# Fox attention of a one-core Trainium2 kernel: new step lists for the last two pairs of heads, and the first output unit closed behind three shares of the second

## What is computed

```
q = q * HEAD_DIM ** -0.5                        # 16 heads of 64
c = cumsum(log_sigmoid(f_logit))                # forget gate, per head
s = q @ k.T + c[query] - c[key], causal         # 512 x 512 scores
o = softmax(s) @ v
m = o @ w_out                                   # w_attn_out, 1024 x 1024
x = x + rmsnorm(m); then the first MLP of the layer
```

## Time and profile before

| what | value |
|---|---|
| time of three runs | 1836.65, 1836.42, 1834.61 us; median 1836.42 |
| the profiled execution's own time | 1832.28 us |
| its span | 1830.5 us |
| PE busy | 1757.6 us, 96% of the span |
| DVE, ACT, POOL busy | 1068.9, 740.6, 180.0 us |
| pair 6, pair 7 on PE | from 682.59 to 705.03 us, from 705.03 to 729.25 us |
| output product on PE after the lists | units a and b to 745.6 us, unit 2 from 748.61 us |

### The profile page before, as it was taken

One profiled execution on the slowest core, in us unless ns is written; L12 is line 12 of the kernel. 1 busy time (PEld: TensorE's weight loads), 2 busy tenths in 40 slices (PEclk: granted clock), 3 DMA queues, 4 the chain that ended last, 5 costly groups with the idle time before them and its releaser, 6 DMA issues.

```text
span 1830.5 us, 21934 instructions
## 1 busy us (share of the span) xinstructions
PE 1757.6 (96%) x8332; PEld 1448.3 (79%) x8332; DVE 1068.9 (58%) x1397; ACT 740.6 (40%) x1076; POOL 180.0 (10%) x144
## 2 busy tenths in 40 slices
PE   8999999999899998999999999979998999999987
PEld 6978877888688887768888887768886888888866
DVE  6367777676556776484435353776556635444475
ACT  4256764665425666351212123642124312222245
POOL 2000110000300000130000001430004000000041
PEclk9999999999999999999999999989999999999999
DMA  7222123214223221222332222322321333222221
GB/s 238 92 69 69 37 69 95 63 54 138 70 81 93 69 70 42 81 92 94 99 106 92 92 92 81 104 69 92 102 79 64 119 103 99 92 92 94 96 65 57
DMA packets 164702, 160.26 MB, mean 88 GB/s; under 512 B 13873, under 2 KB 157518, under 8 KB 164366
## 3 DMA queue, kind: packets, MB, share of 16 engines
q1 hardware_dynamic: 164622, 159.16, 27.8%
HBM read 150.36 MB, written 4.19 MB: 84 GB/s over the span
## 4 chain that ended last, share of the span: by engine, by line
PE 69%; issue 13%; DVE 7%; POOL 5%; ACT 4%; DMA 2%; SPq 0%; POOLq 0%; DVEq 0%; ACTq 0%
PE bank L749 21%; PE bank L751 21%; PE bank L750 21%; POOL ssum L2404 3%; PE bank L1009 2%; PE bank L1021 1%; DVE split_weights L1737 1%; DVE work L1796 1%; POOL tmp L2437 1%; DVE act_a L1783 1%; ACT split_weights L1248 1%; DMA raw_weights<-in_w_mlp_up 1%; DMA raw_weights<-in_w_ple_gate 1%; ACT sq L1278 1%; POOL ssum L2408 0%
## 5 line engine op out<-in xcount | busy, mean ns | idle before, releaser
L749 PE MATMUL bank<-act_a,split_weights 128*128 128x512 f32 x1392 | 558.0, 401 | 32.6 <-DVE act_a L1783 24.1
L751 PE MATMUL bank<-act_a,split_weights 128*128 128x512 f32 x1392 | 547.9, 394 | 0.0
L750 PE MATMUL bank<-act_a,split_weights 128*128 128x512 f32 x1392 | 547.8, 394 | 0.0
L1248 ACT ACTIVATE split_weights<-raw_weights 128x2048 fp32r<-128x2048 f32 (+1 forms) x118 | 221.8, 1880 | 335.8 <-PE bank L751 335.7
L1737 DVE TENSOR_TENSOR split_weights<-raw_weights,split_weights 128x2048 fp32r<-128x2048 f32 (+1 forms) x118 | 273.2, 2316 | 123.1 <-ACT split_weights L1248 119.7
L749 PEld LDWEIGHTS bank<-act_a,split_weights 128*128 128x128 f32 x1392 | 264.0, 190 | 96.5 <-issue 23.1
L751 PEld LDWEIGHTS bank<-act_a,split_weights 128*128 128x128 f32 x1392 | 263.8, 190 | 57.7
L750 PEld LDWEIGHTS bank<-act_a,split_weights 128*128 128x128 f32 x1392 | 264.4, 190 | 53.6 <-issue 2.2
L749 PE MATMUL bank<-act_b,split_weights 128*128 128x512 f32 x664 | 260.4, 392 | 0.0
L750 PE MATMUL bank<-act_b,split_weights 128*128 128x512 f32 x664 | 258.4, 389 | 0.0
L751 PE MATMUL bank<-act_b,split_weights 128*128 128x512 f32 x664 | 258.4, 389 | 0.0
(11 more groups left out here) (191 smaller groups left out, 2073.8 us busy)
## 6 DMA issues: line engine op xcount, KB each, us to landing
raw_weights<-in_w_mlp_up SPq DMA_DIRECT2D x32, 1024.0 KB, 5.4
raw_weights<-in_w_mlp_down SPq DMA_DIRECT2D x32, 1024.0 KB, 5.1
raw_weights<-in_w_in SPq DMA_DIRECT2D x20, 1024.0 KB, 5.3
raw_weights<-in_w_conv_in SPq DMA_DIRECT2D x12, 1024.0 KB, 5.1
raw_weights<-in_w_attn_in SPq DMA_DIRECT2D x16, 512.0 KB, 4.7
raw_weights<-in_w_ple_gate SPq DMA_DIRECT2D x8, 1024.0 KB, 5.1
raw_weights<-in_w_out SPq DMA_DIRECT2D x4, 1024.0 KB, 5.1
raw_weights<-in_w_attn_in SPq DMA_DIRECT2D x4, 1024.0 KB, 5.5
```

The costliest lines, as they stand in the source:

```text
L749: nc.tensor.matmul(dst, w[0], a[0], start=first, stop=False)
L750: nc.tensor.matmul(dst, w[0], a[1], start=False, stop=False)
L751: mm = nc.tensor.matmul(dst, w[1], a[0], start=False, stop=last)
L1248: nc.scalar.activation(wsp[:, pl.slot, 0, pl.split_cols], raw[:, pl.slot, pl.raw_cols], ACT.Copy)\
```

## The change

The four NEAR and LAST lists of PE, ACT and DVE (six lists in all) are written anew, with the same steps in another order; `w` and `c` stand earlier in them. `mixer_out` takes two shares of unit b, `turn_p`, a third share of b, share 7 of a, and then shares 3 to 7 of b. And `split_share` counts up a new semaphore `w_begun` with ACT's first half, so that DVE's `c0` and `c1` wait for the first half alone and `c2` for the second; this holds for all pairs of Fox and MLA.

```diff
--- before.py
+++ after.py
@@ -333,7 +333,7 @@
             ATT[kind] = {n: sem(f"{kind}_{n}") for n in (
                 "stage_hi", "staged", "scores", "turned", "clipped", "softplus", "masked", "part_hi",
                 "part_ready", "summed", "w_exp", "negmax", "exp", "normed", "pt_hi", "pt_ready",
-                "v_hi", "v_staged", "out", "sum_log", "sum_inverse", "gathered", "gated", "o_hi", "o_ready")}
+                "w_begun", "v_hi", "v_staged", "out", "sum_log", "sum_inverse", "gathered", "gated", "o_hi", "o_ready")}
         halves_copied = [sem("halves_copied0"), sem("halves_copied1")]
 
         block = ctx.enter_context(nc.Block())
@@ -384,14 +384,14 @@
         DVE_FOX = "m0 m1 c0 c1 m2 y0 p0 m3 m4 p1 c2 s2 c3 p2 p3 m5 m6 m7 y1 p4 p5 g0 p6 p7 x0 x1 s3 g1"
 
 
-        PE_NEAR = "z0 g0 z1 z2 g1 t0 g2 t1 t2 z3 z4 z5 g3 t3 z6 g4 v0 t4 g5 t5 g6 z7 g7 t6 t7 v1"
-        ACT_NEAR = "y0 e0 y1 e1 e2 p0 p1 e3 p2 p3 w0 e4 e5 r0 p4 w1 p5 e6 e7 p6 p7 s2 r1"
-        DVE_NEAR = "m0 m1 m2 y0 p0 m3 p1 p2 p3 m4 m5 y1 g0 c0 m6 p4 m7 p5 x0 x1 p6 p7 c1 s2 c2 g1 c3"
-
-
-        PE_LAST = "z0 z1 z2 g0 t0 z3 t1 g1 z4 t2 z5 g2 t3 z6 g3 t4 z7 v0 t5 g4 t6 t7 g5 g6 v1"
-        ACT_LAST = "o0 s1 o1 e0 w0 e1 p0 y0 o2 e2 p1 o3 e3 o4 p2 e4 p3 w1 o5 e5 o6 y1 e6 p4 p5 e7 r0 p6 p7 r1"
-        DVE_LAST = "o0 m0 m1 o1 s1 m2 p0 o2 m3 p1 m4 m5 y0 o3 o4 p2 p3 m6 c0 m7 c1 o5 p4 p5 c2 y1 o6 g0 p6 p7 g1 c3"
+        PE_NEAR = "z0 z1 z2 g0 g1 t0 t1 z3 g2 z4 t2 z5 g3 t3 z6 g4 t4 t5 v0 g5 z7 g6 g7 t6 t7 v1"
+        ACT_NEAR = "y0 e0 e1 p0 p1 e2 w0 w1 e3 p2 p3 e4 e5 e6 p4 p5 y1 r0 e7 p6 p7 s2 r1"
+        DVE_NEAR = "m0 m1 m2 m3 p0 y0 c0 c1 p1 p2 m4 m5 p3 m6 c2 p4 y1 m7 p5 g0 x0 x1 p6 p7 c3 s2 g1"
+
+
+        PE_LAST = "z0 z1 z2 t0 z3 g0 t1 g1 t2 g2 t3 z4 z5 z6 g3 t4 z7 g4 v0 t5 g5 t6 t7 g6 v1"
+        ACT_LAST = "o0 o1 e0 s1 p0 e1 y0 e2 o2 e3 p1 o3 w0 p2 y1 o4 p3 e4 o5 w1 e5 o6 e6 e7 p4 p5 r0 p6 p7 r1"
+        DVE_LAST = "m0 o0 m1 m2 o1 p0 m3 s1 o2 y0 p1 o3 c0 p2 m4 o4 y1 p3 o5 m5 c1 m6 m7 c2 c3 p4 p5 o6 g0 p6 p7 g1"
 
         ACT_MLA_LAST = "e0 e1 y1 p0 e2 p1 w0 e3 p2 p3 w1 e4 e5 p4 o0 e6 p5 o1 e7 p6 r0 p7 o2 r1"
         DVE_MLA_LAST = "m0 m1 m2 m3 p0 p1 p2 m4 p3 m5 c0 c1 c2 y1 m6 p4 c3 m7 p5 o0 p6 g0 o1 p7 x0 x1 o2 g1"
@@ -1106,12 +1106,13 @@
                     begun = sum(w == "g" for w, _ in steps(PE_LAST))
                     a, b = (Place(tab, name, j) for j in range(2))
                     b_banks = [bank(b, m) for m in range(2)]
-                    for share in range(begun):
+                    for share in range(2):
                         beside(b, share, tab.extra[name], ready[0], b_banks)
                     turn_p()
+                    beside(b, 2, ready=ready[0], dst=b_banks)
                     for share in range(begun, KT):
                         beside(a, share, ready=ready[0])
-                    for share in range(begun, KT):
+                    for share in range(3, KT):
                         beside(b, share, ready=ready[0], dst=b_banks)
                     project_normed(name, x, first=2)
                 else:
@@ -1248,15 +1249,14 @@
                 nc.scalar.activation(wsp[:, pl.slot, 0, pl.split_cols], raw[:, pl.slot, pl.raw_cols], ACT.Copy)\
                     .then_inc(w_hi, 1)
 
-            def split_share(pl, share):
+            def split_share(pl, share, begun):
 
                 if share == 0:
                     act.wait_ge(raw_landed[pl.slot], pl.landed)
                     act.wait_ge(tile_done, pl.freed)
                 cols = slice(share * UNIT // 2, (share + 1) * UNIT // 2)
-                hi = nc.scalar.activation(wsp[:, pl.slot, 0, cols], raw[:, pl.slot, cols], ACT.Copy)
-                if share:
-                    hi.then_inc(w_hi, 1)
+                nc.scalar.activation(wsp[:, pl.slot, 0, cols], raw[:, pl.slot, cols], ACT.Copy)\
+                    .then_inc(w_hi if share else begun, 1)
 
             def split_half(name, j, half):
 
@@ -1509,7 +1509,7 @@
                                 act.wait_ge(tile_read, here.tile)
                             stage_values(kind, pair + s // 2, s % 2, A["v_hi"])
                         elif what == "w":
-                            split_share(ahead, s)
+                            split_share(ahead, s, A["w_begun"])
                         elif what == "o":
                             output_hi(kind, s)
                         elif what == "r":
@@ -1737,9 +1737,11 @@
                 V.tensor_tensor(wsp[:, pl.slot, 1, cols], raw[:, pl.slot, pl.raw_cols], wsp[:, pl.slot, 0, cols].bitcast(F32),
                                 ALU.subtract).then_inc(w_split, 1)
 
-            def split_share(pl, share):
+            def split_share(pl, share, begun):
 
                 if share == 0:
+                    dve.wait_ge(*begun)
+                elif share == 2:
                     dve.wait_ge(w_hi, pl.u + 1)
                 cols = slice(share * UNIT // 4, (share + 1) * UNIT // 4)
                 lo = V.tensor_tensor(wsp[:, pl.slot, 1, cols], raw[:, pl.slot, cols], wsp[:, pl.slot, 0, cols].bitcast(F32),
@@ -2122,7 +2124,7 @@
                         elif what == "m":
                             maxima(pair, s)
                         elif what == "c":
-                            split_share(ahead, s)
+                            split_share(ahead, s, (A["w_begun"], pair + 1))
                         else:
                             turned_lo(pair, s)
 
```

## The result

The changed kernel takes 1820.95 us (median of 6 runs, 1819.67 to 1821.85) beside 1836.14 us of the kernel before (6 runs, 1834.61 to 1836.65). The ratio is 0.9919, with a 95% interval of 0.9906 to 0.9932: 14.9 us less, 12.5 to 17.3.

The account below looks back on a forecast made before the run. The prediction took PE as the bound, with gain only where it waits or its clock falls. Terms of 3.0, 3.2, 0.5 and 0 summed to 6.7 us, from the median 1836.42 to 1829.7 us; range 1825.8 to 1833.0.

Parts of the forecast that it names:

- Term A: Behind pair 7's last v1: c3 placed ahead of p4 lets unit b start at once; 3.0 us gained.
- Term B: In mixer_out: unit a closed early, five shares of b cover the wait ahead of unit 2; 3.2 us gained.
- Term C: Seam of pairs 6 and 7: shorter waits less new small ones; 0.5 us gained in sum.
- the walk: Step-by-step timing of the new lists of pairs 6 and 7; found new waits of some 0.3 and 0.5 us.
- Term D: Clock fall in pair 7: between 0 and 1.7 us to gain; 0 taken.
- rival 1: The clock does not fall in pair 7: gain 8.4 us, 1828.0 us; chance 0.30.
- The added waits: One more DVE wait per pair, for w_begun, over twelve pairs: 0.8 us at most, 0 taken.
- Rival 2: Share 7 of a comes before tile 7 is ready, holding b's shares 3 to 7: 1832.7 us; chance 0.10.
- Rival 3: Gain taken back at the first MLP's loads, or hidden by scatter: no change, 1836.4 us; chance 0.08.
- Rival 4: Earlier splits in pairs 6 and 7 hold ACT's and DVE's chain: 3.1 us slower, 1839.5 us; chance 0.05.

Follow-up runs that it names:

- e7: The changed kernel with DVE's c3 of the last pair put back at the end of its list; 1824.61 us, ratio to before 0.9945.
- e3: The kernel before with the new order of shares in mixer_out alone; 1829.94 us, ratio to before 0.9973.
- e4: The changed kernel with the old order of mixer_out; 1825.39 us, ratio to before 0.9946.
- e6: The changed kernel with w_begun waited for in pairs 6 and 7 only, elsewhere c0 waits for both halves; 1823.21 us, ratio to before 0.9935.
- e8: The changed kernel, unedited, measured again as a reference; 1821.24 us, ratio to before 0.9922.
- e9: The changed kernel with share g7 of pair 6 laid between t7 and v1; 1820.29 us, ratio to before 0.9924.
- e11: The changed kernel with g7 of pair 6 behind t7, o0 split in pair 6 and g0 ahead of t0 in pair 7; 1820.0 us, ratio 0.9919.
- e12: The changed kernel with share 0 of unit a in pair 6 between t7 and v1, pair 7 beginning with share 1; 1821.64 us, ratio 0.9921.
- e13: The kernel before with 45 useless matmuls laid into three PE stalls, ahead of pair 7's first share, unit b and unit 2; 1833.0 us, ratio 0.9987.
- e2: The kernel before with the semaphore w_begun alone, old lists and old mixer_out; 1832.9 us, ratio to before 0.9987.
- the control: An unchanged copy of the kernel before, measured beside it; 1835.34 us, ratio 0.9997.
- e5: The kernel before with m2 moved ahead of c0 and c1 in DVE_FOX, no new semaphore; 1834.4 us, ratio 0.9993.

## Why the prediction was right or wrong

**Term A (3.0 us): right.** The distance from the last `v1` matmul to unit b went from 3.13 to 0.12 us. e7 gives the wait back by moving `c3` alone.

**Term B (3.2 us): right.** Unit 2 starts 3.2 us sooner behind b's last matmul, and tile 7 is ready in time: no wait on it between b's shares. e3 takes only this edit and loses the wait, e4 gives it back (3.1 us).

**Term C (0.5 us): right in size.** The seam stall is 1.72 us (forecast 1.7), the copy's wait is gone, `g2` waits 0.3 us as the walk found. Two small items came out otherwise. The wait of `v1` in pair 6 stays whole (forecast 0.2 less), and the pair is 0.1 us shorter elsewhere. `v1` of pair 7 lost 0.24 us (forecast 0.5): it starts 0.47 us behind its forerunner instead of 0.23, of which 0.07 us show as idle. The load of unit 2 went 8.5 us sooner by the clock of the span, of which some 4 us are the shorter stretches ahead of it.

**Term D (0 taken, 1.7 us kept for the range): wrong, rival 1 was the case.** A stall of 1.72 us in the same place left the clock up, here and in e4, e6, e7, e8 and e9; the falls of e11 (700.5 us) and e12 (709.4 us) came behind other stalls, of 1.84 and 2.16 us. But the reason why 1.7 us could be won is not the prediction's. It counted 0.07 x 24.2 us as lost to the fall; by e13 the old order lost nothing by it, because the copy of head 15 held PE just as long. The 1.7 us became free only because the change also moved that copy out of the way.

**The added waits (0 taken): right.** With twelve waits more the MLA pairs take 21.95 us as before, and no Fox pair is longer by more than 0.02 us.

**The step that failed is in the paragraph on the added wait: "the earlier quarters in the MLA pairs and Fox pairs 0 to 5 can give back little, because PE waits there for 0.2 us and 0.4 us. I take 0 for this too".** For the MLA pairs it held (21.95 us a pair in both). For Fox pairs 0 to 5 it cost 3.0 us: e2 gains them with the semaphore alone, e6 loses them without it there. The waits of PE are not a bound on what it loses, since a matmul is drawn 0.39 us long at a distance of 0.23. The number to read was the length of a pair: in the trace of before the distance from pair 0 to pair 1 is 20.60 us and each later one 21.2 to 21.4, with the same lists. The 12.3 us of DVE's idle in the earlier trace rows pointed at the place, but not at the price: six of the ten cases are Fox pairs with 1.49 us each, of which pair 0 loses nothing, three are MLA pairs with 0.96 us each, which lose nothing, and the last is 0.5 us in pair 6.

**The second step is the base: "That execution was 4.1 us faster than the median of the runs, and I put the change against the median".** The prediction took the gain to be the same against both. It was not. The profiled execution had one of the three falls that the control shows, and neither profile of the changed kernel has any there. The two that the trace of before did not show are 3.4 us. Neither step alone takes the time out of the range: 6.7 + 3.0 us gives 1826.7 us. With rival 1 as well it is 1825.0 us, and with the two falls 1821.6 us, beside 1820.95 measured.

**The sum.** A 3.0, B 3.2, C 0.5, the early pairs 3.0, three falls about 5.1: 14.8 us, against 14.9 measured (12.5 to 17.3). From the profiles the same: pair 7 to the 3850th matmul 60.5 - 48.7 = 11.7 us (from the unrounded values) against the control, of which A, B, C's 0.3 in pair 7 and the falls are 11.6. The sum needs three falls in the median execution of before; with the one of the profiled execution it is 11.4 us, and the two profiles, of before and of after, are 11.6 us apart. So the number of falls is the least certain term. e13 seems to speak against counting the first fall, since it was swallowed by the copy there; in the changed kernel that wait is gone, and the gain of its removal is the same 1.7 us under another name.

**The rivals.** Rival 2: tile 7 was in time. Rival 3: the stretch behind unit 2 took back 0.7 us, not the gain, and even those can't be told from scatter: in the profiles of e1 to e12 that stretch takes 1067.9 to 1069.5 us, with the old lists and the new. Rival 4: PE's shares covered the earlier splits; in pair 7's window ACT was busy 18.60 us of 25 and DVE 17.54, and the only new waits of PE are the small ones named under term C.

**What stays open.** Why the same stall brings a fall in one execution and not in another: before and its copy have the same three waits, and one and three falls. How often which number comes was not counted, since only profiled executions show it; so the clock's part of the gain rests on one execution each of the control, e13 and the edits, and on two of the changed kernel. The lists of pairs 6 and 7 without the semaphore were not tried: with the old wait `c0` at its new place would need ACT's second half, which stands behind steps that wait for it.

## What to carry to other kernels

Where matmuls are pipelined, read what PE loses from the distances of starts, and compare stretches that have the same list: a pair that takes 21.3 us where its neighbour takes 20.6 has 0.7 us to give, whatever the waits say. When an engine stands idle at a wait and the next steps of the critical engine come from behind that wait in its queue, look at a finer semaphore too: here it gave 3.0 us in the trace, where moving one step past the wait gave 0.5 us, because the work behind the wait then came late for the next step. And before a profiled execution is used as the base of a sum, look at what it did differently from the median: each of the two long stalls was here worth 3 us of waiting and up to 1.7 us of clock, and the profile showed a fall at one stall of three, where it cost nothing.

## What the hardware did that I had not expected

Seven profiles (before, e1 to e5, e7) hold 16 stalls of PE of 2.4 to 3.1 us between 700 and 760 us. Behind 11 of them the granted clock fell to 0.50, in the control at 1.7 to 1.8 us each; behind 5 it stayed at 1.00, among them the 2.85 and the 3.06 us of the profiled execution of before. Each of the 5 came later in a profile whose first stall had its fall; the three falls of the control and of e2 show that this is no rule either. Four of the 11 falls began within the stall, 0.2 to 0.9 us ahead of its end. Shorter stalls went either way too: 2.16 us in e12 and 1.84 us in e11 had a fall, 2.17 us in e13 and 1.84 us in e9 had none. Filling the three stalls with 45 matmuls that compute nothing removed all falls and made the kernel faster, 0.9987 [0.9978, 0.9996]. The Trainium skill (TensorE: Matmul & The Clock Gate, Why this matters for your kernels) asks for no long idle gaps of PE between bursts of matmuls. e13 agrees that the gaps matter; but stalls of 2.36 us had falls here, shorter than the gaps that the page warns of, and the measurement decides.
